# The memory's keys and values projected from its columns ahead of the norm, in the prologue of a one-layer decoder trunk

## What is computed

```python
h = rms_norm(x, norm_mix)
m = rms_norm(mem, norm_mem)              # mem (256, 1024): row * rsqrt(mean square) * gain
km, vm = split_cols(m @ w_kv, (512, 512))
scores = einsum('bthd,bmhd->bhtm', xq, km) * 128 ** -0.5
out = einsum('bhtm,bmhd->bthd', softmax(scores), vm)
```

## Time and profile before

| | us |
|---|---|
| median of 3 runs | 2588.87 |
| lowest and highest run | 2584.39, 2591.76 |
| the profiled execution | 2587.02 |
| its span, first to last instruction | 2585.2 |
| PE busy in the span | 2533.5 |
| mean granted TensorE clock | 0.998 |

### The profile page before, as it was taken

How to read it: one execution, slowest core, us unless ns; L and a number is a source line. 1 busy time by engine, 2 the same in 40 slices (tenths; PEclk the granted TensorE clock), 3 DMA queues, 4 the chain that set the end, 5 groups by cost and what they waited for, 6 DMA issues and landing times.

```text
span 2585.2 us, 34664 instructions
## 1 busy us (share of the span) xinstructions
PE 2533.5 (98%) x11968; PEld 2118.9 (82%) x11968; DVE 1536.7 (59%) x2253; ACT 1205.3 (47%) x1752; POOL 452.9 (18%) x411
## 2 busy tenths in 40 slices
PE   7999999999999999999999999999999999999998
PEld 6888887888788888888878888888887888888886
DVE  4457467665656636566646664656665565465666
ACT  4544344544454525455454443544445444354544
POOL 4144444000004510000001541000000254000000
PEclk9999999999999999999999999999999999999999
DMA  8522468444522132543442213255443222344443
GB/s 284 156 90 66 158 208 286 173 129 147 181 66 71 61 114 82 195 147 131 137 158 66 82 50 114 98 179 163 146 136 126 66 66 77 103 136 158 147 161 132
DMA packets 191896, 338.96 MB, mean 131 GB/s; under 512 B 7041, under 2 KB 119041, under 8 KB 183521
## 3 DMA queue, kind: packets, MB, share of 16 engines
q1 hardware_dynamic: 188784, 327.92, 38.3%
q10 hardware_dynamic: 2928, 8.66, 0.8%
HBM read 311.39 MB, written 25.17 MB: 130 GB/s over the span
## 4 chain that ended last, share of the span: by engine, by line
issue 49%; PE 40%; DVE 4%; POOL 4%; ACT 2%; DMA 1%; SPq 1%; DVEq 0%; ACTq 0%; POOLq 0%
PE banks L1593 10%; PE banks L1595 10%; PE banks L1594 10%; PE banks L1749 3%; PE banks L1729 1%; POOL queries L700 1%; DVE w_lo L1122 1%; POOL h_lo L725 1%; PE banks L1790 1%; PE banks L1773 1%; PE banks L1788 1%; POOL rstd L658 1%; DVE u_lo L1500 1%; ACT w_hi L761 1%; DVE sr L1332 0%
## 5 line engine op out<-in xcount | busy, mean ns | idle before, releaser
L1593 PE MATMUL banks<-h_hi,w_hi 128*128 128x512 f32 (+1 forms) x1728 | 667.5, 386 | 10.6 <-DVE w_lo L1122 3.6
L1595 PE MATMUL banks<-h_hi,w_lo 128*128 128x512 f32 (+1 forms) x1728 | 659.1, 381 | 0.0
L1594 PE MATMUL banks<-h_lo,w_hi 128*128 128x512 f32 (+1 forms) x1728 | 659.0, 381 | 0.0
L1122 DVE TENSOR_TENSOR w_lo<-raw,w_hi 128x2048 fp32r<-128x2048 f32 x144 | 349.2, 2425 | 297.7 <-ACT w_hi L761 297.7
L761 ACT ACTIVATE w_hi<-raw 128x2048 fp32r<-128x2048 f32 x144 | 275.5, 1913 | 269.6 <-PE banks L1593 230.1
L1593 PEld LDWEIGHTS banks<-h_hi,w_hi 128*128 128x128 f32 x1728 | 324.9, 188 | 77.1 <-issue 16.3
L1595 PEld LDWEIGHTS banks<-h_hi,w_lo 128*128 128x128 f32 x1728 | 324.8, 188 | 63.2
L1594 PEld LDWEIGHTS banks<-h_lo,w_hi 128*128 128x128 f32 x1728 | 325.0, 188 | 60.7
L1593 PE MATMUL banks<-w_hi,u_hi 128*128 128x512 f32 x896 | 351.8, 393 | 0.0
L1595 PE MATMUL banks<-w_hi,u_lo 128*128 128x512 f32 x896 | 349.1, 390 | 0.0
L1594 PE MATMUL banks<-w_lo,u_hi 128*128 128x512 f32 x896 | 348.8, 389 | 0.0
(11 more groups left out here) (170 smaller groups left out, 3224.3 us busy)
## 6 DMA issues: line engine op xcount, KB each, us to landing
raw<-in_w_up SPq DMA_DIRECT2D x64, 1024.0 KB, 5.4
raw<-w_mix SPq DMA_DIRECT2D x64, 1024.0 KB, 4.8
raw<-in_gla_w_in SPq DMA_DIRECT2D x57, 1024.0 KB, 5.0
raw<-in_w_down SPq DMA_DIRECT2D x48, 1024.0 KB, 4.7
raw<-in_w_out SPq DMA_DIRECT2D x24, 1024.0 KB, 5.0
xin<-in_x SPq DMA_DIRECT2D x5, 2048.0 KB, 10.9
xin<-in_w_down SPq DMA_DIRECT2D x10, 1024.0 KB, 4.9
w_mix<-xin SPq DMA_DIRECT2D x10, 1024.0 KB, 10.3
```

The costliest lines, as they stand in the source:

```text
L1122: nc.vector.tensor_tensor(w_lo[:, i % 2, :], raw[:, i % 2, :], w_hi[:, i % 2, :].bitcast(F32), ALU.subtract).then_inc(lo_split.sem, PIECES)
L1593: after_chunk(pe.matmul(to, left[0], right[0], start=start, stop=False, skip_group_check=goes_on))
L1594: pe.matmul(to, left[0], right[1], start=False, stop=False, skip_group_check=goes_on)
L1595: return pe.matmul(to, left[1], right[0], start=False, stop=stop, skip_group_check=goes_on)
```

## The change

- A second input, `mem_columns`, holds the memory transposed. It is loaded in two halves of four 128-row blocks (`memory`, in the place of `mem_lo`), alternating with the two halves of weight chunk 0. ACT and DVE make `memory_hi` and `memory_lo` from it straight, with the gain; the memory's 16 transposes, and its norm ahead of the products, are gone.
- Keys and values are projected from the un-normed memory. Keys of chunk 0 are made in two halves of the contraction. The two keys of a chunk stand beside each other with those of the next chunk in banks 6 and 7, the values in banks 4 and 5, each read once at the end.
- The memory's rows are loaded later into `xres`, behind the second half of x; ACT squares them behind high part 3 of x, DVE and POOL make the root, POOL two diagonal matrices of it, PE one product with a matrix of ones that spreads the root over all partitions (bank 3). DVE multiplies the keys by it, ACT scales the values by the root, both behind the eight parts of x.
- x is loaded in two halves of two tiles; squares and scaling follow each half. Transposes 0 and 1 of x stand between the values of chunk 2 and 3; 2 and 4 behind the first group of chunk 3, 3 and 5 behind the second, then 6 and 7.
- The six small transfers of w_gate2 are issued by ACT ahead of everything it computes; the constants on SP come last before the loop's chunk 0.

The core of the diff:

```diff
 def early_uses():
+    for f in range(2):
+        yield 6 + f, ("km", f)
+    for m in range(MT):
+        yield 4 + m, ("vm", m)
     for k in range(KD):
         yield k % 2, ("x0T", k)
+    yield 3, "memory rstd"
...
+            for p, landed in enumerate((first_half_loaded, raw_loaded[0].sem)):
+                at = slice(p * KD // 2, (p + 1) * KD // 2)
+                sp.dma_start(memory[:, at, :], mem_cols[:, at, :]).then_inc(memory_loaded[p], 16)
+                sp.dma_start(as_kblocks(raw, 0, KD)[:, at, :], wkv[:, at, 0:FCOLS]).then_inc(landed, 16)
+            load_kv(1)
+            sp.dma_start(xin[:, 0:2, :], x_tiles[:, 0:2, :]).then_inc(first_x_loaded, 16)
+            load_kv(2)
+            sp.dma_start(xin[:, 2:4, :], x_tiles[:, 2:4, :]).then_inc(xin_loaded.sem, 16)
+            load_kv(3)
+            sp.dma_start(xres[:, 0:MT, :], mem_tiles).then_inc(mem_loaded, 16)
...
+            pool.wait_ge(first_consts_loaded, 16 * 3)
+            for m in range(MT):
+                pool.wait_ge(*rstd_ready.early(TILES + m))
+                nc.gpsimd.tensor_tensor(memory_diag[:, m * P:(m + 1) * P], ident[:],
+                                        rstd[:, 0, m:m + 1].broadcast_to([P, P]), ALU.mult)\
+                    .then_inc(memory_diag_ready, 1)
...
             act.wait_ge(first_consts_loaded, 16 * 3)
+            for p in range(2):
+                act.wait_ge(memory_loaded[p], 16)
+                for k in range(p * KD // 2, (p + 1) * KD // 2):
+                    nc.scalar.activation(memory_hi[:, k, :], memory[:, k, :], ACT.Copy,
+                                         scale=gain_mem[:, k:k + 1]).then_inc(hi_part.sem, 1)
...
+                at = slice(p * CHUNK // 2, (p + 1) * CHUNK // 2)
+                nc.scalar.activation(w_hi[:, 0, at], raw[:, 0, at], ACT.Copy).then_inc(hi_split.sem, 1)
             first_split_hi(1)
...
+            act.wait_ge(first_x_loaded, 16)
+            for t in range(2):
+                square(1, t, xin)
+            first_split_hi(2)
+            act.wait_ge(*xin_loaded.early(0))
+            for t in range(2, TILES):
+                square(1, t, xin)
+            first_split_hi(3)
+            for k in range(KD // 2):
                 first_x_high(k)
+            act.wait_ge(mem_loaded, 16)
+            for m in range(MT):
+                square(0, m, xres)
+            first_split_hi(KV_CHUNKS)
+            act.wait_ge(consts_loaded, 16 * 6)
+            act.wait_ge(w2_loaded, 16 * (3 * PAIR // RANK))
+            nc.scalar.activation(w2_parts[:], w2_raw, ACT.Copy)
+            nc.scalar.activation(wg_pair[:, :, 0:RANK], wg_raw, ACT.Copy).then_inc(wg_hi_ready, 1)
+            for k in range(KD // 2, KD):
+                first_x_high(k)
+            act.wait_ge(*early_full("memory rstd"))
+            nc.scalar.activation(memory_rstd, bank("memory rstd")[:, 0:MEM], ACT.Copy)\
+                .then_inc(bank_read[bank_of("memory rstd")], 1)
...
+            for k in range(KD // 2):
+                first_x_low(k)
+            for m in range(MT):
+                dve.wait_ge(*ssq_ready.early(TILES + m))
+                mean_square(0, m)
+            first_split_lo(KV_CHUNKS)
+            dve.wait_ge(consts_loaded, 16 * 6)
...
+            for k in range(KD // 2, KD):
+                first_x_low(k)
+            dve.wait_ge(*early_read("memory rstd"))
+            for f in range(2):
+                dve.wait_ge(*early_full(("km", f)))
+                nc.vector.tensor_tensor(kmT[:, f:XH:2, :], heads_of(bank(("km", f)), 2),
+                                        memory_rstd.unsqueeze(1).broadcast_to([P, 2, MEM]), ALU.mult)\
+                    .then_inc(bank_read[bank_of(("km", f))], 1)
...
+            memory_keys(0)
+            memory_keys(1)
+            for m in range(MT):
+                memory_values(0, m)
+            for k in range(2):
                 first_x_transposes(k)
+            for m in range(MT):
+                memory_values(1, m)
+                for k in (2 + m, 4 + m):
+                    first_x_transposes(k)
+            for k in range(6, KD):
+                first_x_transposes(k)
+            pe.wait_ge(ones_set, 1)
+            pe.wait_ge(memory_diag_ready, MT)
+            pe.matmul(bank("memory rstd")[:, 0:MEM], ones[:], memory_diag, start=True, stop=True)\
+                .then_inc(bank_full[bank_of("memory rstd")], 1)
             pe.wait_ge(wg_ready, 1)
```

More of the change, by code:

```diff
@@ L342, in build @@
             mem_hi = mx("mem_hi", [P, XH, BLOCK], F32R)
-            mem_lo = mx("mem_lo", [P, XH, BLOCK], F32R)
+            with ExitStack() as low:
+                mem_lo = low.enter_context(nc.sbuf_tensor("mem_lo", [P, XH, BLOCK], F32R))
+            memory = mx("memory", [P, KD, MEM])
             sr = mx("sr", [P, KD, BLOCK])
@@ L809, in first_x_high @@
                                      scale=gain_mix[:, k:k + 1]).then_inc(hi_part.sem, 1)
[L811 to L826, removed]
-                    nc.scalar.activation(w2_parts[:], w2_raw, ACT.Copy)
-                    nc.scalar.activation(wg_pair[:, :, 0:RANK], wg_raw, ACT.Copy).then_inc(wg_hi_ready, 1)
@@ L832, in _ @@
+            for m in range(MT):
+                act.wait_ge(*early_full(("vm", m)))
+                act.wait_ge(*rstd_ready.early(TILES + m))
+                nc.scalar.activation(vm[:, m, :], bank(("vm", m)), ACT.Copy, scale=rstd[:, 0, m:m + 1])\
+                    .then_inc(bank_read[bank_of(("vm", m))], 1)
             with act.Fori(0, BLOCKS) as n:
@@ L1207, in _ @@
-            for k in range(MT, KD):
-                first_x_low(k)
+            x_norm(range(2))
+            first_split_lo(2)
+            x_norm(range(2, TILES))
+            first_split_lo(3)
+            for k in range(KD // 2):
+                first_x_low(k)
+            for m in range(MT):
[3 more added lines that the diff above has]
+            dve.wait_ge(consts_loaded, 16 * 6)
+            nc.vector.tensor_scalar(half_gain_o[:], gain_o[:], 0.5, None, ALU.mult).then_inc(half_gain_ready, 1)
@@ L1662, in _, with memory_keys @@
-            for k in range(MT, KD):
-                first_x_transposes(k)
+            def memory_keys(i):
+                wh, wl = as_kblocks(w_hi, i, KD), as_kblocks(w_lo, i, KD)
+                for half in range(2):
+                    pe.wait_ge(*hi_split.early(PIECES * i + half))
+                    pe.wait_ge(*lo_split.early(PIECES * i + half))
+                    for f in range(2):
+                        for k in range(half * KD // 2, (half + 1) * KD // 2):
+                            if i == 0 and f == 0:
+                                pe.wait_ge(memory_low, k + 1)
+                            last = product(bank(("km", f))[:, i * MEM:(i + 1) * MEM],
+                                           (wh[:, k, f * P:(f + 1) * P], wl[:, k, f * P:(f + 1) * P]),
+                                           (memory_hi[:, k, :], memory_lo[:, k, :]), k == 0, k == KD - 1)
+                        if i == 1 and half == 1:
+                            last.then_inc(bank_full[bank_of(("km", f))], 1)
+                chunk_done()
@@ new lines, in memory_values @@
+            def memory_values(i, m):
+                wh, wl = as_kblocks(w_hi, i, KD), as_kblocks(w_lo, i, KD)
+                if m == 0:
+                    pe.wait_ge(*hi_split.early(last_piece(2 + i)))
+                    pe.wait_ge(*lo_split.early(last_piece(2 + i)))
+                at = slice(m * P, (m + 1) * P)
+                for k in range(KD):
+                    last = product(bank(("vm", m))[:, i * FCOLS:(i + 1) * FCOLS],
+                                   (memory_hi[:, k, at], memory_lo[:, k, at]), (wh[:, k, :], wl[:, k, :]),
+                                   k == 0, k == KD - 1)
+                if i == 1:
+                    last.then_inc(bank_full[bank_of(("vm", m))], 1)
+                chunk_done(m == MT - 1)
@@ L2047 @@
         give(name, a)
+    give("mem_columns", columns(np.asarray(inputs["mem"])[0]))
     out = nc.dram_tensor("out", (SEQ, D), F32, kind="ExternalOutput").ap()
```

167 lines of the change are left out of this document (57 added, 110 removed).

## The result

The changed kernel takes 2594.55 us (median of ten runs; lowest 2589.84, highest 2596.30), the kernel before 2589.39 (2583.32 to 2591.76). The ratio is 1.0022, 95% interval 1.0014 to 1.0030: 5.7 us slower, between 3.6 and 7.8, so within 0.3%, the forecast's side (the two medians lie 5.2 us apart). The profiled execution took 2596.3 (span 2594.5) at a mean granted clock of 0.996. It is the slowest one of its kernel: the two traces lie 9.3 us apart.

What follows compares the result with a forecast made beforehand. The matmul engine, busy 98%, bounds the kernel; only the loop's start can move. -3.4 (last product) + 4.2 (tail) + 2.5 (clock) + 0.5 (port) = +3.8 us, on median 2588.9 giving 2592.7, range 2587 to 2598.

Steps and rivals of the forecast that it cites:

- the port: Prologue tail: POOL's mix sums meet DVE's low split and lengthen it, 0.5 us, between 0 and 1.2.
- the clock: Loop start: PE's long idle drops it to 1.2 GHz; 2.5 us including transpose 6, slow stretch 1.5 to 3.0.
- The start: Prologue up to the first memory product: 3.9 us earlier, at 10.45 instead of 14.31, 0.6 either way.
- The middle: Memory products up to the last one: end 3.4 us earlier, at 39.2 against 42.55.
- The order on ACT: Prologue tail: squares, split and constants stand behind high part 3, which needs transpose 3, made after the last product.
- rival (b): ACT's order does not hold the tail back, which stays 7.5 us; -3.9 to -5, some 2584.5; chance 0.06.
- The tail: From the last product to the loop's first matmul: 11.7 us against 7.5, so 4.2 longer.
- PE's idle: Prologue tail, from transpose 5 to transpose 6 of x: PE idle about 6.7 us.
- The transfers on SP: Moved loads of x's second half, memory rows and constants lie between 13 and 28 us, needed after 21 and 40: free.
- Rival (c): Clock returns late in the loop; from 15 us at half speed, slower by 7.8 us, 2597 and more; chance 0.08.
- Rival (d): Change doesn't run ahead: first product not before 14.3 us; +7.7, 2596.6; chance 0.07.
- (a): Early start pays, clock not falling or only shortly, splits on time; -2 to +1, some 2588; chance 0.17.

Runs made afterwards that it cites:

- e6: Changed kernel plus 28 small unread products on PE ahead of the memory's first product; ratio 1.0028 to the kernel before.
- e4: Changed kernel with x's transposes 2 and 3 between the two value groups of chunk 3, 4 to 7 behind both; ratio 1.0006 to the kernel before.
- e1: Changed kernel with POOL's mix sums held until transposes 6 and 7 of x are read; ratio 1.0023 to the kernel before.
- e7: Changed kernel plus 84 unread products on PE between transposes 5 and 6 of x; ratio 1.0019 to the kernel before.
- e3: Changed kernel with the memory's squares and mean squares ahead of high part 0 of x; ratio 1.0017 to the kernel before.
- e2: Changed kernel plus 56 unread products on PE between transposes 5 and 6 of x; ratio 1.0020 to the kernel before.
- e11: e9 with ACT first waiting only for gain_mem, and w_gate2 issued behind the split of chunk 1; median 2579.3, ratio 0.9964 to the kernel before.
- e10: Changed kernel with only the gates' constants moved, ahead of x's high part 0 on ACT and low part 0 on DVE; ratio 1.0014 to the kernel before.
- e9: e5 with the gates' constants ahead of x's high part 0 on ACT and low part 0 on DVE; median 2580.5, ratio 0.9969 to the kernel before.
- e8: e5 plus warming products, ACT first waiting only for gain_mem, and w_gate2 issued behind the split of chunk 1; ratio 0.9995 to the kernel before.
- e5: e4 with ACT and DVE reordered: squares, x parts 0 and 1, split, constants, parts 2 to 7; ratio 0.9994 to the kernel before.

## Why the prediction was right, and where it was not

The forecast was 2592.7 in a range of 2587 to 2598; the median is 2594.55. The forecast case came about: it runs ahead, the tail eats it up, the loop starts at half clock. The sum was made against a profiled execution, as +3.8 us; the measured difference is 5.7 (3.6 to 7.8). In the two traces a date past the slow stretch, ACT's first copy of xq_a, moved from 55.77 to 63.16, by 7.4 us. The terms that were off account for it: 3.8, plus 1.3 for the last product, plus 3.3 for the port, less 1.3 for the clock, is 7.1.

The number is better than its terms. The port and the clock both fell outside their own bounds, 3.8 for 0 to 1.2 and 1.2 for 1.5 to 3.0, in opposite directions; with the clock as priced the sum would have been 8.4, past the +7 of the bounds. And the loop's first matmul, named as near 51.5, came at 56.70: 1.3 of the 5.2 us are the last product, 3.3 the port, the rest mostly transposes 6 and 7 at half clock (1.97 us for 1.03). By its steps:

- **The start, right to 0.8 us.** ACT began at 7.22, inside 6.15 to 7.4; I took 6.8. Six issues cost 3.36, not 2.7, so the table load came at 5.64. The gains were there 0.3 us behind it. The rest, 4.0 us to the first product, I had at 3.65.
- **The middle, right.** The 27 slow products cost 2.4 us (I took 2.3), the wait ahead of transpose 4 was 1.57 (1.6), the splits of chunks 2 and 3 were done at 24.4 and 30.2 (24 and 30). The last product ended at 40.49, not 39.2; 0.8 of that is the start. But a price is not a gain: e6 took the slow products away and got back less than half.
- **The order on ACT, right**, and with it the verdict on rival (b). e4 shows the cause: 5.1 us from moving transposes alone.
- **The tail was mis-sized: 16.2 us from the last product to the loop, not 11.7.** The term that failed is the port, 0.5 us, "between 0 and 1.2". It came to 3.8 (e1). I priced only the one operation that the earlier trace rows show in a meeting, the low split, and left the three behind it at their undisturbed 1.1 us, without a reason. The loss does not go by the size of what waits but by the size of what it waits for. A rule that I cited would have said so. The Trainium skill's "SBUF — State Buffer" ("SBUF: two separate sides") calls the port that VectorE and GpSimd share an exclusive lock, held for the whole instruction, and takes in DVE operations with two SBUF inputs (against a GpSimd operation that reads SBUF) as well as those in a 2-port mode. The trace agrees, with half_gain_o at 1.22 for 0.16; I should have asked it of each operation in the stretch. Low parts 4 and 5 read one operand from PSUM and kept 1.40 beside POOL's sums.
- **The clock, over-priced: 1.2 us (e7), not 2.5.** It did fall, and longer than thought: the window of 45 to 57 us stands at 0.50, 1.2 GHz. But PE had next to nothing to do in it. The advice against idle gaps in the Trainium skill's "TensorE: Matmul & The Clock Gate" ("Why this matters for your kernels") is borne out by the fall behind this one, yet what the low clock cost was only the work that fell in it.
- **PE's idle** was 10.36, not 6.7: nearly all of the difference is the port's 3.8 us.
- **The transfers on SP, free as forecast.** scan_mask held the queue for 4.22 us at 19.70, and no engine of the path waited for it. The memory's rows, first used at 41.71, had landed by 28.2 us in e3, where ACT waits for them. The split of the loop's chunk 1, late at 57.95, cost PE no wait.
- **Rival (c)** would have needed 15 us of half clock under full load. The stretch was nearly that long (from some 44.5 us, where the clock leaves 1.00, to about 58.4 in PE's pace), but mostly empty. **Rival (d)** fell by the first product at 11.23, **(a)** by the idle.

What stays open: the prediction named a difference in the loop itself as a sign of being wrong, and there is one. From the first copy of xq_a to the end it is 2529.4 us in before's trace and 2531.3 in after's, 1.9 us more, of which PE's waits behind 62 us show 1.4 (25.0 for 23.6). The traces of e2 to e11 have 0.8 to 2.5 us more than before, that of e1, with its wait of 3.3, 3.6. Before has one trace, and executions of one kernel differ by 6 to 8 us for reasons that no run here shows, so it can't be told whether this belongs to the change. For the same reason the 7.4 us of the two traces and the 5.7 of the ratio can't be brought together more closely.

## What to carry to other kernels

When work is moved, look at what the other user of a shared port will be doing at its new place, for every operation in the stretch, the smallest first: each can cost a whole operation of the other engine. Ahead of a wait on the path put nothing in program order that can stand anywhere else, and check that work moved off one stretch doesn't meet something later, as e1's sums did. A gain at the head of a chain (an earlier first product, products at full pace) can be worth little until the next supply, here the splits and the tail, is moved with it: e6 got back 0.9 us of 2.4 at x's first transpose, and nothing that the ratio shows.

## What the runs showed of the hardware

- A DVE operation of two elements for a partition took 1.22 us beside POOL's sums and 0.16 without them; one of 32 x 512 took 1.71 and 0.68, one of 128 x 128 took 1.26 and 0.29. POOL lost too: 3.31 for 1.27 us when the low split was ahead of it.
- How long PE stays slow after its first product differs between traces of kernels with the same head: products are 0.21 us apart for 3.3 us in e10 (10.98 to 14.26), for 6.1 in e9 (11.14 to 17.22) and after (11.23 to 17.30), at a granted clock of 1.00. Of the 1.46 us between x's first transpose in e10 (29.75) and after (31.21), 1.2 come from this. With one trace each, whether it goes by kernel or by execution stays open.
- The length of one idle does not by itself decide whether the granted clock falls. It stayed at 1.00 behind 1.13 us (e9), 1.57 (after, at 37.13), 1.94 (e8, at 24.42) and 2.19 (e6, at 11.19), and fell behind 2.26, 3.35 (e8, at 41.26) and 3.92 (e5). In e1 it fell at about 42.9 us, only 0.3 us after transposes that had followed an idle of 1.56.
- Issuing six transfers of 32 KB on ACT's queue took 3.36 us at the head, with ACT computing nothing, and 4.72 from 12.07 us on in e8, where the split of chunk 1 that had just begun ran beside it (12.05 to 13.97) and ACT then stood still until 16.89. In e11 the same six at the same place took 2.80.
